# The order of the first block in a fused decoder step: input rows, weight splits and constants rearranged

## The reference, cut to what matters

```python
h = rms_norm(x, norm_g)                       # 1024 prompt rows + 64 sample rows, 1024 columns
z = jnp.einsum('bsd,de->bse', h, w_in)        # here in blocks of 512 columns
qb = rms_norm(z_qb.reshape(b, s, B_HEADS, 2, HEAD_DIM), q_norm_b)   # first block
kb = rms_norm(z_kb.reshape(b, s, B_HEADS, 2, HEAD_DIM), k_norm_b)   # second block
lam = exp(sum(lambda_q1 * lambda_k1)) - exp(sum(lambda_q2 * lambda_k2)) + lam_init
```

## Time and profile before

| | |
|---|---|
| median of 3 runs | 1908.26 us (1905.12 to 1911.16) |
| profiled execution | 1910.81 us, of which 1908.8 us are the span |
| PE busy | 1681.4 us, 88% of the span |
| POOL, DVE, ACT busy | 680.1, 707.4 and 599.8 us |
| mean granted TensorE clock | 0.938 of full speed |

### The profile page before, as it was taken

One profiled execution on the slowest core, in us unless ns is written; L12 is line 12 of the kernel. 1 busy time (PEld: TensorE's weight loads), 2 busy tenths in 40 slices (PEclk: granted clock), 3 DMA queues, 4 the chain that ended last, 5 costly groups with the idle time before them and its releaser, 6 DMA issues.

```text
span 1908.8 us, 38064 instructions
## 1 busy us (share of the span) xinstructions
PE 1681.4 (88%) x14552; PEld 1371.5 (72%) x14552; DVE 707.4 (37%) x1751; ACT 599.8 (31%) x1393; POOL 680.1 (36%) x971
## 2 busy tenths in 40 slices
PE   4899698999899998999989779796879878789798
PEld 3677465788799998999977557574657646568587
DVE  4321266322272223622154433343344243358511
ACT  3321265422163222622152332333233233212200
POOL 3654311256443555345472310212121210266420
PEclk8999899999899998999989889798899988889899
DMA  4147400465515565265325757868678676655232
GB/s 150 45 153 266 156 24 21 159 214 186 186 42 197 208 219 186 58 229 193 106 77 186 256 189 241 265 230 283 210 265 259 230 264 230 199 172 195 92 120 83
DMA packets 164252, 336.24 MB, mean 176 GB/s; under 512 B 29873, under 2 KB 50738, under 8 KB 162674
## 3 DMA queue, kind: packets, MB, share of 16 engines
q1 hardware_dynamic: 142514, 212.86, 34.3%
q10 hardware_dynamic: 21568, 121.04, 18.0%
HBM read 294.05 MB, written 127.07 MB: 221 GB/s over the span
## 4 chain that ended last, share of the span: by engine, by line
PE 76%; issue 6%; DMA 5%; POOL 5%; DVE 3%; ACT 2%; SPq 2%; ACTq 0%; DVEq 0%; POOLq 0%
PE ps L1809 16%; PE ps L1810 15%; PE ps L1811 15%; PE ps L2004 4%; PE ps L1948 4%; DMA raw<-in_w_in 3%; PE ps L1899 3%; PE ps L1968 3%; PE ps L2046 3%; POOL w_lo L876 2%; PE ps L1955 2%; PE ps L1807 2%; PE ps L1808 2%; PE ps L2029 2%; PE ps L1920 1%
## 5 line engine op out<-in xcount | busy, mean ns | idle before, releaser
L1809 PE MATMUL ps<-w_hi,hT 128*128 128x512 f32 x1168 | 487.6, 417 | 27.9 <-issue 14.0
L1810 PE MATMUL ps<-w_lo,hT 128*128 128x512 f32 x1168 | 471.8, 404 | 0.0
L1811 PE MATMUL ps<-w_hi,hT 128*128 128x512 f32 x1168 | 471.6, 404 | 0.0
L876 POOL TENSOR_TENSOR w_lo<-raw,w_hi 128x512 fp32r<-128x512 f32 x145 | 185.6, 1288 | 436.0 <-ACT w_hi L1065 435.8
L1809 PEld LDWEIGHTS ps<-w_hi,hT 128*128 128x128 f32 x1168 | 275.1, 236 | 67.3 <-issue 18.3
L1811 PEld LDWEIGHTS ps<-w_hi,hT 128*128 128x128 f32 x1168 | 274.5, 235 | 37.6
L1810 PEld LDWEIGHTS ps<-w_lo,hT 128*128 128x128 f32 x1168 | 275.4, 236 | 33.2
L1546 DVE STREAM_TRANSPOSE k_in<-k_in 128x512 f32<-128x512 f32 x232 | 151.2, 689 | 129.2 <-DMA k_in<-in_cache_b_kv 69.8
L1065 ACT ACTIVATE w_hi<-raw 128x512 fp32r<-128x512 f32 x153 | 95.4, 630 | 266.5 <-DMA raw<-in_w_in 246.9
L969 POOL COPY q_rep<-qTs 32x96 f32<-32x96 f32 (+1 forms) x256 | 59.3, 232 | 212.9 <-issue 115.3
L856 POOL TENSOR_TENSOR rs<-ss,half_pow 128x8 f32<-128x8 f32 (+3 forms) x81 | 127.0, 1568 | 6.7
(11 more groups left out here) (217 smaller groups left out, 2583.7 us busy)
## 6 DMA issues: line engine op xcount, KB each, us to landing
out<-in_cache_a_kv ACTq DMA_DIRECT2D x32, 2040.0 KB, 9.3
k_in<-in_cache_b_kv SPq DMA_DIRECT2D x128, 256.0 KB, 4.0
v_in<-in_cache_b_kv SPq DMA_DIRECT2D x128, 256.0 KB, 4.8
raw<-in_w_in SPq DMA_DIRECT2D x104, 256.0 KB, 4.0
k_in<-in_cache_a_kv SPq DMA_DIRECT2D x104, 256.0 KB, 5.9
v_in<-in_cache_a_kv SPq DMA_DIRECT2D x104, 256.0 KB, 4.3
out<-in_cache_a_kv ACTq DMA_DIRECT2D x8, 2016.0 KB, 9.5
raw<-in_w_in ACTq DMA_DIRECT2D x40, 256.0 KB, 5.7
```

The costliest lines, as they stand in the source:

```text
L876: pool.tensor_tensor(lo, raw[:, q % 4, :], hi.bitcast(F32), ALU.subtract).then_inc(lo_done, 1)
L1809: pe.matmul(z, hi, wh, start=first, stop=False)
L1810: pe.matmul(z, hi, wl, start=False, stop=False)
L1811: return pe.matmul(z, lo, wh, start=False, stop=last)
```

## The change

- **SP:** the load of row tile 0 goes ahead of the identity and the gain; of the 12 constants the four pieces of the query gains keep their place (with a semaphore of their own, `s_const`), the other eight move to step 7 of block 0.
- **ACT:** squares of tiles 0 and 1, then weight chunk 0, then the high parts of row tile 0; the square of tile i + 4 stands in step i between the two high parts of tile i + 3.
- **POOL:** 1/rms of tile i + 4 between the two low parts of tile i + 3, both behind `rs` of tile i; no weight splits in block 0.
- **DVE:** gain, splits and scaling interleaved in the start; in step i the first gain half of tile i + 3 goes between the head sums and `zn`, then the weight split of chunk i (new here), the second gain half, and the scaling of tile i + 4. The lambda terms move to steps 1 and 4 of block 1, ACT's exponential to step 2 of block 1.
- **PE:** a chunk waits for the low half of the rows that it uses, in place of both; the wait for `h_hn` 4 goes to ACT's first square of `z`; in tile 0 the turns of tile 2 stand behind chunks 4 and 7, not 1 and 5.

```diff
-        N_CONST = 16 * 12
+        N_CONST = 16 * 8
...
-            sp.dma_start(ident[:, :], c_ident).then_inc(first_in, 16)
-            sp.dma_start(gcol[:, :], norm_g[0].rearrange("(c p) -> p c", p=P), allow_slow_non_contiguous=True).then_inc(first_in, 16)
...
             load_x(0)
+            sp.dma_start(ident[:, :], c_ident).then_inc(first_in, 16)
+            sp.dma_start(gcol[:, :], norm_g[0].rearrange("(c p) -> p c", p=P), allow_slow_non_contiguous=True).then_inc(first_in, 16)
             load_x(1)
...
             for col, vec in ((0, qna), (1, qnb)):
                 for h in range(2):
                     sp.dma_start(qcol[h * HD:(h + 1) * HD, col:col + 1],
-                                 vec[0].rearrange("(d o) -> d o", o=1)).then_inc(const_in, 16)
-            for col, vec in ((0, kna), (1, knb)):
-                sp.dma_start(krow[:, col, :], vec[0].partition_broadcast(P)).then_inc(const_in, 16)
-            for col, vec in enumerate((lq1, lk1, lq2, lk2)):
-                sp.dma_start(lamv[:, col, :], vec[0].partition_broadcast(P)).then_inc(const_in, 16)
-            sp.dma_start(coef[:, :], c_coef).then_inc(const_in, 16)
-            sp.dma_start(subrow[:, :], subln[0].partition_broadcast(P)).then_inc(const_in, 16)
-
+                                 vec[0].rearrange("(d o) -> d o", o=1)).then_inc(s_const, 16)
+
+            def constants():
+                for col, vec in ((0, kna), (1, knb)):
+                    sp.dma_start(krow[:, col, :], vec[0].partition_broadcast(P)).then_inc(const_in, 16)
+                for col, vec in enumerate((lq1, lk1, lq2, lk2)):
+                    sp.dma_start(lamv[:, col, :], vec[0].partition_broadcast(P)).then_inc(const_in, 16)
+                sp.dma_start(coef[:, :], c_coef).then_inc(const_in, 16)
+                sp.dma_start(subrow[:, :], subln[0].partition_broadcast(P)).then_inc(const_in, 16)
...
+                    if u == 0 and i == NT - 1:
+                        constants()
                     if i < KC:
                         load_chunk(u + 1, i)
...
-            def input_lo(i):
-                for half in range(2):
-                    j = 2 * i + half
-                    pool.wait_ge(h_hi, j + 1)
+            def input_lo(i, half):
+                if i < TILES:
+                    pool.wait_ge(h_hi, 2 * i + half + 1)
...
-                if q == KC:
+                if q == 2 * KC:
                     pool.wait_ge(lo_done, q)
...
-            def input_step(i):
+            def input_rstd(i):
                 if i < TILES:
...
-                if 1 <= i <= TILES:
-                    input_lo(i - 1)
-
-            for i in range(3):
-                input_step(i)
+
+            input_rstd(0)
+            input_rstd(1)
+            input_lo(0, 0)
+            input_lo(0, 1)
+            input_rstd(2)
+            input_lo(1, 0)
+            input_lo(1, 1)
+            input_rstd(3)
+            input_lo(2, 0)
+            input_lo(2, 1)
 
...
-                    if u == 0:
-                        input_step(i + 3)
                     if kind in "qk":
...
+                    if u == 0:
+                        input_lo(i + 3, 0)
+                        input_rstd(i + 4)
+                        input_lo(i + 3, 1)
+                    if u == 1 and i == 0:
+                        pool.wait_ge(const_in, N_CONST)
...
-                    if i < KC:
+                    if i < KC and u:
                         split_lo(u + 1, i)
...
-            def input_hi(i):
-                for half in range(2):
-                    j = 2 * i + half
-                    act.wait_ge(h_hn, j + 1)
+            def input_hi(i, half):
+                if i < TILES:
+                    act.wait_ge(h_hn, 2 * i + half + 1)
...
-            def input_step(i):
-                r = nrows(i)
+            def input_square(i):
...
-                if 1 <= i <= TILES:
-                    input_hi(i - 1)
-
-            for i in range(3):
-                if i == 2:
-                    for k in range(4):
-                        split_hi(0, k)
-                input_step(i)
+
+            input_square(0)
+            input_square(1)
+            split_hi(0, 0)
+            input_hi(0, 0)
+            input_hi(0, 1)
+            for k in range(1, 4):
+                split_hi(0, k)
+            input_hi(1, 0)
+            input_square(2)
+            input_hi(1, 1)
             for k in range(4, KC):
                 split_hi(0, k)
-            act.wait_ge(setup, 2)
-            act.activation(lam[:, 2:4], lam[:, 0:2], ACT.Exp).then_inc(setup, 1)
+            input_hi(2, 0)
+            input_hi(2, 1)
+            input_square(3)
...
-                    act.wait_ge(setup, 4)
+                    act.wait_ge(setup, 1)
...
-                    if u == 0:
-                        input_step(i + 3)
-                    elif i in COPY_AT and len(COPY_AT) * (u - 1) + COPY_AT.index(i) < N_COPIES:
+                    if u and i in COPY_AT and len(COPY_AT) * (u - 1) + COPY_AT.index(i) < N_COPIES:
...
+                        elif m == 0:
+                            act.wait_ge(h_hn, 4)
                         act.activation(bank(5 + m % 2)[0:r], z, ACT.Square).then_inc(sq_ready, 1)
...
+                    if u == 0:
+                        input_hi(i + 3, 0)
+                    if u == 1 and i == 2:
+                        act.wait_ge(setup, 3)
+                        act.activation(lam[:, 2:4], lam[:, 0:2], ACT.Exp).then_inc(setup, 1)
                     if i < KC:
                         split_hi(u + 1, i)
+                    if u == 0:
+                        input_square(i + 4)
+                        input_hi(i + 3, 1)
...
-                r = nrows(i)
-                dve.wait_ge(h_rs, i + 1)
-                dve.tensor_scalar(xn[0:r, i % 2, :], xt[0:r, i % 2, :], rs_x[0:r, i % 2, 0:1], None, ALU.mult)\
...
-            def input_gain(i):
-                r = nrows(i)
-                for half in range(2):
-                    j = 2 * i + half
+                if i < TILES:
...
+            def input_gain(i, half):
+                if i < TILES:
+                    r, j = nrows(i), 2 * i + half
                     dve.wait_ge(h_t, j + 1)
...
-            def input_step(i):
-                if i < TILES:
-                    rows_scale(i)
-                if 1 <= i <= TILES:
-                    input_gain(i - 1)
-
-            for i in range(3):
-                if i == 2:
-                    for k in range(4):
-                        split_lo(0, k)
-                input_step(i)
+            rows_scale(0)
+            rows_scale(1)
+            input_gain(0, 0)
+            input_gain(0, 1)
+            split_lo(0, 0)
+            split_lo(0, 1)
+            input_gain(1, 0)
+            split_lo(0, 2)
+            input_gain(1, 1)
+            split_lo(0, 3)
+            rows_scale(2)
             for k in range(4, KC):
                 split_lo(0, k)
-
-            dve.wait_ge(const_in, N_CONST)
-            for j in range(2):
-                dve.tensor_tensor_reduce(out=lamv[:, 2 * j, :], in0=lamv[:, 2 * j, :], in1=lamv[:, 2 * j + 1, :],
-                                         scale=1.0, scalar=0.0, op0=ALU.mult, op1=ALU.add,
-                                         accum_out=lam[:, j:j + 1]).then_inc(setup, 1)
-            dve.wait_ge(setup, 3)
-            link(dve.tensor_tensor(lam[:, 4:5], lam[:, 3:4], lam[:, 2:3], ALU.subtract))
-            link(dve.tensor_scalar(lam[:, 5:6], lam[:, 4:5], -LAM_INIT, None, ALU.add))
-            link(dve.tensor_scalar(subrow[:, :], subrow[:, :], 1.0 - LAM_INIT, None, ALU.mult))
-            link(dve.scalar_tensor_tensor(out=coef[:, 0:1], in0=coef[:, 1:2], scalar=lam[:, 5:6],
-                                          in1=coef[:, 0:1], op0=ALU.mult, op1=ALU.add))
-            dve.tensor_scalar(qcol[:, :], qcol[:, :], -(HD ** -0.5), None, ALU.mult).then_inc(setup, 1)
+            input_gain(2, 0)
+            input_gain(2, 1)
+            rows_scale(3)
+
+            def lambda_products():
+                dve.wait_ge(const_in, N_CONST)
+                for j in range(2):
+                    dve.tensor_tensor_reduce(out=lamv[:, 2 * j, :], in0=lamv[:, 2 * j, :], in1=lamv[:, 2 * j + 1, :],
+                                             scale=1.0, scalar=0.0, op0=ALU.mult, op1=ALU.add,
+                                             accum_out=lam[:, j:j + 1]).then_inc(setup, 1)
+
+            def lambda_rest():
+                dve.wait_ge(setup, 4)
+                link(dve.tensor_tensor(lam[:, 4:5], lam[:, 3:4], lam[:, 2:3], ALU.subtract))
+                link(dve.tensor_scalar(lam[:, 5:6], lam[:, 4:5], -LAM_INIT, None, ALU.add))
+                link(dve.tensor_scalar(subrow[:, :], subrow[:, :], 1.0 - LAM_INIT, None, ALU.mult))
+                link(dve.scalar_tensor_tensor(out=coef[:, 0:1], in0=coef[:, 1:2], scalar=lam[:, 5:6],
```

(50 more changed lines are left out.)

## The result

The changed kernel takes 1890.59 us (median of 4 runs, 1889.22 to 1893.31), the kernel before 1906.69 in the same comparison; the ratio is 0.9909, 95% interval 0.9884 to 0.9934. That is 16.1 us faster, clear of no change but under 1%. The profiled execution took 1889.22, with a span of 1887.4, which is 21.4 under the earlier trace rows; the profiled execution of the kernel before (1910.81) was 4.1 us above its median here and this one 1.4 under its own, so the 21.4 and the 16.1 do not contradict each other.

What follows compares the result with a forecast made beforehand. PE, held by waits in block 0, was taken as the bound. Block 0's end falls from 101.05 to 80.5, gaining 20.5, less 0.8 for the clock, net 19.7; from the median 1908.26 that gives 1888.5, range 1882 to 1897.

Steps and rivals of the forecast that it cites:

- landmark: PE's turn of `zn` after tile 8, which closes block 0: forecast at 80.5 us instead of 101.05.
- the clock: TensorE's lower level, 1.2 in place of 2.4 GHz, after the 3 us wait in tile 1: 0.8 us set against the gain.
- the likeliest case: The forecast itself: gain 17 to 22 us, time 1886 to 1891, chance 0.58.
- The ring in its new order: Block 0's per-tile chain over ACT, DVE and POOL to PE's second half: 6.7 us instead of 9.09, under PE's 7.1.
- Rival A: Block 0's chain of ACT, DVE and POOL binds, not PE: 8.0 or 9.09 per tile, gain 15 or 10; chance 0.22.
- The first product: PE's first matmul in tile 0 of block 0: could go at about 13.3 us, not 19.15.
- tile 0's end: PE's end of the first row tile in block 0: near 24.7 us, where it was 37.4.
- The splits: DVE's weight splits 4 to 7 in block 0's start, beside two POOL low parts: done at 24.0 us.
- The hole in tile 1: PE's wait in block 0 for scaling 3, before the turn of row tile 3 at 29.6: 3 us.
- The gain should pass through whole: Behind block 0, loads and copies move with block 1's start: block 2's first product near 142, 20 us earlier.
- Rival B: Loads in block 1 take the gain back before block 2 or attention b: 1903 to 1911, chance 0.08.
- Rival C: Low TensorE clock for over half of block 0 makes the kernel slower, about 1940 if for all; chance 0.03.

Runs made afterwards that it cites:

- experiment 3: Changed kernel with block 1's weight splits back on POOL, behind the second low part of each step: ratio 0.9922 to the kernel before.
- experiment 5: Changed kernel with POOL's two low parts of tile 2 ahead of 1/rms of tile 3: 1891.59 us, one execution.
- experiment 2: Kernel before with only the constants and lambda terms moved into block 0's end and block 1: ratio 0.9943 to the kernel before.
- experiment 1: Changed kernel with the eight constants and the whole lambda work back at the start: ratio 0.9943 to the kernel before, median 1897.8 us.
- experiment 4: Changed kernel with the start order of before on ACT and DVE; loops, constants and PE as changed: ratio 0.9893 to the kernel before.
- experiment 7: Changed kernel with PE's part undone (waits for both low halves, tile 2's turns behind chunks 1 and 5): 1885.24 us in one execution; timed again, ratio 0.9911.
- 8: Changed kernel with only the turns of tile 2 back behind chunks 1 and 5 of tile 0, waits by halves kept: 1892.86 us, one execution.
- 11: The changed kernel run again, unedited: ratio 0.9903 to the kernel before, median 1889.3 us.
- experiment 9: Changed kernel with ACT's and DVE's old start order, row tile 3 loaded ahead of query gains, tile 0's gains ahead of scaling 1: ratio 0.9894.
- experiment 10: Changed kernel with PE's part undone, row tile 3 loaded ahead of the query gains and squared ahead of tile 2's high parts: ratio 0.9883, median 1886.2 us.
- 6: Changed kernel with 14 extra products, result dropped, in tile 1's wait ahead of the turn of (3,0): 1883.68 us, one execution.

## Why the prediction was right, and where it was off

**Block 0.** Forecast was a landmark of 80.5 plus 0.8 for the clock, 81.3; it is 82.97 and 83.12. The last turn moved by 18.1, against a net 19.7. The time was forecast at 1888.5 and is 1890.59. That it lies in the likeliest case's range (1886 to 1891) has a little luck in it: the kernel before was 1.6 us faster in this comparison than the 1908.26 that the forecast started from, and the gain between the medians, 16.1, is just under the 17 to 22 of that case.

**The tiles.** The ring in its new order was worked out at 6.7, under PE's 7.1. PE does set the pace: square to `zn` is 3.39 (44.96 to 48.35), the split behind it takes 1.37 because a low part runs beside it, and PE waits for nothing. The margin of 0.4 is not to be seen, though: the split ends at 50.51, PE's second half at 50.42, and the gain starts at 50.45, so ring and PE arrive together, at 6.9. Turns stand 6.9 apart, 0.2 less than the term had. From tile 1's end to the landmark it is 45.1, reckoned 45.8. Rival A did not come; with the weight split back on POOL (experiment 3) the ring costs 1.2 us in all, where A had 4.5. By the missing margin it was closer than that.

**The start.** The first product (13.3 against 13.02) and tile 0's end (24.7 against 25.4) were close, the second in part because two errors met. The splits were reckoned to end at 24.0 (from 18.7, although scaling 2 was to hold DVE until 19.55) and ended at 22.3, for the collisions cost less than all four instructions added up. But the nine products from 21.68 on took 3.7 us at the low clock, where at 0.23 each they take 2.1. Two terms were too small. The hole in tile 1 was put at 3 us and is 3.78, because I had a split stand beside a low part but not a scaling: scaling 3 took 1.74, not 0.75 (experiment 5 gives it back its 0.75). Together with tile 0's end, which came 0.7 late, that puts the turn behind the hole at 31.19, not at 29.6. And the clock was put at 0.8: the low level took the second half of tile 0 (granted 0.83 from 20 to 30) and 6.7 us in place of 5.0 for the rest of tile 1. Together these make tile 1 end at 37.88, not at 34.7, 3.2 late; the tiles gave 0.7 and the clock's allowance 0.8 of that back, so the landmark is 1.7 late.

**What the parts are worth.** Of 18.1 us the constants are 6.8 (experiment 2) to 7.8 with about 1 of load in it (experiment 1). The new order of the loops, from tile 1's end on, is 9.6: 54.7 before, 45.1 after. The turn after tile 1 stood here in the kernel before:

```profile
46.31 0.60 PE L1778 MATMUL ps<-ident,zn 128*128 128x128 f32 x4
```

The rest, some 1.7 us, is all that the new start and PE's part leave, and the clock of single executions moves it by as much; and both of them cost against what was there. With the start of before tile 1 ends at 34.43 (experiment 4), with PE's turns of before at 34.6 to 36.1 (experiments 7 and 8), in place of 37.88; up to 1.6 us of each difference are the clock. The prediction had followed the chain (behind chunk 7 the turn of (2,1) waits for the whole tile, and gain (2,1), high part, square 3 and scaling 3 hang on it), and put a hole of 3 us at its end. What it did not ask is what the old places of the turns would give; they bring the turn of (3,0) 1.5 to 1.8 us earlier.

**Behind block 0.** "The gain should pass through whole" holds: block 2 starts 18.2 earlier, attention b 20.1. Rival B did not come. Over all kernels of the study the span's end lies 1799 to 1811 us behind the landmark; that scatter of 12 us, of loads and clock in the other blocks, is why the times tell differences of 3 us in block 0 badly and the landmark tells them better. It is also wide enough for the difference between 16.1 measured and 18.1 in block 0.

**The clock.** Rival C, the low level for over half of block 0, did not come: from 40 us to the end of the block the granted clock is 1.00. By the Trainium skill, TensorE: Matmul & The Clock Gate, Part 1, the level depends on recent activity; the trace agrees in that the low spells lie behind waits, but the length of the wait alone does not decide. In tile 1, waits of 3.78 and 3.79 us had one behind them in all three executions (changed, 3, 11) and 2.62 did (experiment 1), while 3.10 did not (experiment 5), and 2.38 did in one of three (experiments 7 and 8); the same 2.38 just ahead of tile 1 did in experiment 9.

## What to carry to other kernels

Where a chain of small steps on four engines feeds a matmul loop, ask for each step what PE waits for next, not what it waits for first. Here, in experiment 7 the first product came 3.4 us later (16.40 against 13.02) and block 0 still ended earlier, because the scaling of row tile 3 was what PE waited for next. Take loads and constants that nobody needs yet out of the queues ahead of those that somebody does; a wait for the last of twelve small loads cost 7 us. And compare orders by a landmark at the end of the changed stretch, when the rest of the kernel scatters more than the change is worth.

## What the runs showed of the hardware

- VectorE's scaling of 128x1024 (one input in SBUF, 0.75 us alone) takes 1.74 to 1.78 beside a GpSimd subtraction that began just before it (scalings 2 and 3 of the changed kernel, scaling 1 of experiment 9), 1.17 beside one that was half through (experiment 10, 24.63), and 0.75 where the two do not meet. The Trainium skill, SBUF — State Buffer, Who interferes with whom, says of such an instruction in its two-port mode that it stands until the GpSimd one is through. The traces agree to 0.2 us: scaling 3 with the subtraction from 29.32 (1.26 long) would end at 31.3 and ends at 31.13. That it runs in that mode no run here shows.
- The same kernel (experiment 7), profiled twice, had seven products of one tile at the low clock in one execution and none in the other, behind the same 2.38 us wait; that cost 1.5 us.
- The granted clock of a window can miss a low spell near the start: it reads 1.00 from 10 to 20 us in experiments 5 and 6, although products there are 0.43 us apart. The distance of like products tells.
